# Page loads without a loop and a sample tile on four column tiles, in one step of a hybrid decoder

## The chip, the cores and the metric

The kernel runs on one core of one Trainium2 chip. The metric is the device time of one execution in microseconds (us). Three timed runs of the kernel before gave 1723.5, 1726.23 and 1726.19 us; their median is 1726.19 us. Lower is better.

## The reference

One decoder layer handles 1024 prompt tokens and 8 x 4 sample tokens (32 rows). What the change touches is cut out here:

```
def nsa_sample(q, cmp_kv, sel_kv, ..., cache_cmp, cache_sel, win_state, page_table, cmp_w):
    past_cmp = cache_cmp[page_table].reshape(db, past, N_KV, 2, HEAD_DIM)   # 8 sequences x 16 pages of 128 rows
    k_p, v_p = compress_blocks(past_cmp, *cmp_w)                            # blocks of 64 rows -> one key, one value
    o_cmp, imp = compressed_attention(q, k_c, v_c, pos)
    idx, valid = select_blocks(imp, pos)                                    # 16 best blocks by importance
    kv_past = cache_sel[phys, r_past % PAGE_SIZE, gi]                       # pages of the second cache
    ... selected and window attention, gates

def merge_and_ffn(x, conv_out, att_out, ...):
    mix = concat(rmsnorm(conv_out), rmsnorm(att_out)) @ w_out               # (1056, 1024) @ (1024, 1024)
    x = x + mix
    return x + hier_moe(rmsnorm(x, ln2), ...)
```

The page table is a row of 128 integers, 16 for each sample sequence; each names a page of 128 rows in the two caches. Before them stand the input projection (`mix_inputs`) and the convolution module, behind them the experts and the last normalization.

## The kernel before

All data are float32. The program is a row of blocks; at the end of each block all engines meet at a barrier, so a block lasts until its slowest engine is done. Tokens are worked in nine tiles: eight of 128 prompt rows (`NQ` = 8) and a ninth of the 32 sample rows.

1. Input stage, 0 to 321 us. Normalization, projection, convolution taps. GpSimd (POOL) does nothing between two memsets near 1 us and a first copy at 167 us (L609). SyncE (SP) loads inputs; the page table is the DMA of L269, into `page_row`. Near 54 us SP issues its last DMA there and then waits for landings.
2. Compression stage, 321 to 436 us. The 128 pages of `cache_cmp` are 128 KB each (128 partitions x 1 KB). They come in four batches q = 0..3 of 32 pages; `cmp_pages` lets SP load the even 16 and POOL the odd 16 of a batch. Two buffers: batches 0 and 1 go to free memory (batch 1 once the convolution's rows have been turned, `conv_turned`), batch 2 waits for the two products of batch 0 (`compressed` >= 2), batch 3 for those of batch 1 (`compressed` >= 4). SP also loads the weights, 2 MB for keys (`load_weights(0)`) ahead of its batch 0, and 2 MB for values behind it. On TensorE (PE) `compress(q, v)` multiplies a batch with the key weights (v = 0) or the value weights (v = 1), 64 matmul instructions each, L706; `blocks(q)` are small products behind. The order on PE is `compress` for q = 0, 1, 2, then `blocks(0)`, `blocks(1)`, `compress(3, 0)`, `blocks(2)`, `compress(3, 1)`, `blocks(3)`. Between its pages of batch 1 and those of batch 2, POOL does nine additions of 512 columns for the convolution (L831), and ScalarE (ACT) and VectorE (DVE) follow these.
3. Prompt attention, 436 to 732 us. SP loads the 64 pages of `cache_sel` of the first four sequences, POOL the value halves of 16 more.
4. Sample attention, 732 to 832 us, in two halves of four sequences. When the first half's scores stand (`s_scored`), SP loads the key halves of batches 0 and 2 of the second half and POOL those of batches 1 and 3 (`last_pages`, 64 KB a page); the second half's scores (L1279) need all four. When the first half is through (`sampled`), SP, POOL and ACT load the value halves of one batch each.
5. Mix stage, 832 to 1011 us. For each token tile: `turn_mix` transposes, `mix(t, 0)` and `mix(t, 1)` multiply with the left and the right half of `w_out` into PSUM banks 2 and 3 (L1489), DVE's `merge` adds the input row (L1592), ACT takes the squares (L1555), DVE scales (L1615), PE turns the result (`turn_h`, L1499), ACT and DVE copy it (L1564, L1624), PE multiplies with the router (L1511), DVE takes the logits (L1598). The scaled rows of the last tile can only be made when both of its merges are done.
6. Routing, experts and the last normalization, from 1011 us to the end.

A page load works as follows. A register must hold the page number. `value_load` is a load of one integer from `page_row` into a register, with a bounds check and address arithmetic (L645). In `load_pages` a loop runs four times; each round loads four numbers and then issues four DMAs (L648). In batches 2 and 3 the wait for `compressed` stands ahead of the loop, so ahead of the numbers too.

Of the kernel before, what the change touches and what calls it, by code (L numbers as in the profile page):

```python
# [132 lines left out]
def build(nc, a):  # L133

    _, const_at, const_small = const_table()
    with ExitStack() as ctx:
# [109 lines left out]
        tap_place = {what: n for n, what in enumerate([v for us in early_taps for v in us] + late_taps)}  # L246
        with nc.Block() as block:
            @block.sync
            def _(sp):
# [7 lines left out]
                for t in range(TILES):  # L257
# [22 lines left out]
                  .then_inc(sem("state_out"), 16)  # L280
                sp.wait_ge(sem("state_out"), 32)
# [358 lines left out]
        def load_pages(eng, cache, first, b, event, part=slice(0, 256), spare=None):  # L640


            into, step, base = (pages_flat, 256, b * PAGES * 256 + part.start) if spare is None else (spare, 128, 0)
            with eng.Fori(0, PAGES // 4) as s:
                places = [eng.value_load(page_row[0:1, bass.ds(s * 4 + (first + q), 1)],  # L645
                                         min_val=0, max_val=cache.shape[0] - 1) for q in range(4)]
                for q, place in enumerate(places):
                    eng.dma_start(into[:, bass.ds(s * (4 * step) + (base + q * step), part.stop - part.start)],  # L648
                                  cache[bass.ds(place, 1)].rearrange("a p n -> (a p) n")[:, part])\
                       .then_inc(sem(f"{event}{b}"), 16)  # L650
# [15 lines left out]
        pages_flat = flat(A1, 18688)  # L666
# [249 lines left out]
        with nc.Block() as block:  # L916
            @block.sync
            def _(sp):
                for b in range(4):
                    load_pages(sp, a["cache_sel"], b * PAGES, b, "sel_page")  # L920
# [138 lines left out]
            def _(pool):  # L1059
                load_pages(pool, a["cache_sel"], HALF + 3 * PAGES, 3, "sel_values", slice(P, 2 * P), last_values)  # L1060
# [159 lines left out]
        def last_pages(eng, event, part, batches):  # L1220
# [1029 lines left out]
```

## Time and profile before

| what | us |
|---|---|
| timed runs, median of three | 1726.19 |
| the profiled execution, its own time | 1724.38 |
| its span (first to last instruction) | 1722.5 |
| compression stage | 321 to 436 |
| sample attention | 732 to 832 |
| mix stage | 832 to 1011 |
| PE busy in the span | 1418.5 |
| DVE, ACT, POOL busy | 680.9, 371.5, 196.1 |

The profile is of one execution, whose time lies within the three timed ones. Times in rows are us from the start of the span, unless a row says ns. A row of the timeline gives start, duration, engine, line, operation, `out<-in`, shape, count, and in brackets how long the engine had been idle and who ended it. "SPq" and "POOLq" are the instruction sequencers of these engines. PEclk is the clock that was granted to TensorE, 1.00 being 2.4 GHz and 0.50 being 1.2 GHz. "DMA" is the busy share of the core's 16 DMA engines.

### The profile page before, as it was taken

To read this page: it belongs to the slowest core of one execution; us is meant where nothing else is said; L and a number is where in the kernel's file an instruction comes from. 1 tells how busy PE (TensorE), PEld (TensorE's weight loads), DVE (VectorE), ACT (ScalarE), POOL (GpSimd) and SP (SyncE) were. 2 spreads that over 40 slices of the span, in tenths; PEclk is the share of its full clock that TensorE was granted. 3 is DMA by queue.
4 is the path that set the end of the run, shared out by engine and by line. 5 is a ranking of instruction groups with operands and counts; after the bars stand their busy time and mean duration, and the time that the engine had idled before them with its cause. 6 is when DMAs were issued, how large, how long until landed. Compare 5 with 4: busy or idle time off the path is not lost. (4 is left out here: it accounts for less than half of the span.)

```text
span 1722.5 us, 22851 instructions
## 1 busy us (share of the span) xinstructions
PE 1418.5 (82%) x7480; PEld 830.2 (48%) x7480; DVE 680.9 (40%) x1314; ACT 371.5 (22%) x796; POOL 196.1 (11%) x348
## 2 busy tenths in 40 slices
PE   5999999478889888823599942999999999999950
PEld 4665445378656556511355521445444544454420
DVE  3497787501488777645122255001000100010008
ACT  4000111330366554430111100111111111111103
POOL 0000011362100000014000000011111111111111
PEclk8999999788589999966699975999999999999985
DMA  7500000474330000045311107699999999999917
GB/s 267 231 1 6 13 16 19 154 240 123 111 99 14 2 1 2 1 141 146 152 61 61 41 17 302 258 393 401 405 412 386 409 400 402 377 396 395 396 50 291
DMA packets 83021, 326.79 MB, mean 190 GB/s; under 512 B 12319, under 2 KB 48288, under 8 KB 64834
## 3 DMA queue, kind: packets, MB, share of 16 engines
q1 hardware_dynamic: 65130, 287.76, 42.7%
q0 software_dynamic: 15440, 37.09, 6.4%
q10 hardware_dynamic: 2384, 1.06, 0.2%
q8 instruction: 41, 0.67, 0.2%
q14 instruction: 26, 0.21, 0.0%
HBM read 311.20 MB, written 29.45 MB: 198 GB/s over the span
## 5 line engine op out<-in xcount | busy, mean ns | idle before, releaser
L1792 PE MATMUL ps<-arena 128*128 128x512 f32 x544 | 239.9, 597 | 0.0
L1792 PEld LDWEIGHTS ps<-arena 128*128 128x128 f32 x544 | 102.1, 190 | 136.9 <-issue 136.8
L521 DVE SCALAR_TENSOR_TENSOR arena<-arena 128x1024 f32<-128x1024 f32 x120 | 147.5, 1282 | 1.2
L1489 PE MATMUL ps<-arena 128*128 128x512 f32 (+1 forms) x288 | 129.6, 603 | 15.3 <-DVE arena L1584 15.3
L354 PE MATMUL ps<-arena 128*128 128x512 f32 (+1 forms) x384 | 141.2, 527 | 0.0
L1800 PE MATMUL ps<-arena 128*64 128x256 f32 x1088 | 121.2, 380 | 0.0
L308 PE MATMUL ps<-arena 128*128 128x352 f32 x384 | 117.5, 467 | 4.3 <-issue 3.9
L1844 PE MATMUL ps<-arena 128*128 128x512 f32 x272 | 119.6, 591 | 0.0
L1090 ACT ACTIVATE arena<-ps,arena 128x640 f32<-128x640 f32 (+7 forms) x128 | 89.9, 703 | 108.9 <-DVE arena L1167 101.9
L354 PEld LDWEIGHTS ps<-arena 128*128 128x128 f32 x384 | 72.0, 189 | 67.2 <-issue 61.6
L999 PE MATMUL ps<-arena 128*128 128x128 f32 x528 | 87.3, 289 | 20.4 <-DVE arena L1185 9.8
L1904 DVE TENSOR_TENSOR arena<-arena,ps 128x512 f32<-128x512 f32 x17 | 11.7, 689 | 226.8 <-PE ps L1792 226.8
L1800 PEld LDWEIGHTS ps<-arena 128*64 128x64 f32 x1088 | 75.9, 135 | 50.5 <-issue 12.9
L706 PE MATMUL ps<-arena 128*128 128x128 f32 (+1 forms) x512 | 69.2, 299 | 33.5 <-DMA arena<-in_cache_cmp 32.4
L308 PEld LDWEIGHTS ps<-arena 128*128 128x128 f32 x384 | 73.7, 193 | 46.5 <-issue 6.6
L1167 DVE TENSOR_REDUCE arena<-ps 128x1 f32<-128x640 f32 (+7 forms) x128 | 90.6, 708 | 4.4
L1489 PEld LDWEIGHTS ps<-arena 128*128 128x128 f32 (+1 forms) x288 | 51.5, 184 | 80.8 <-issue 80.7
L706 PEld LDWEIGHTS ps<-arena 128*128 128x128 f32 x512 | 68.3, 207 | 34.4 <-issue 34.3
L1013 PE MATMUL ps<-arena 128*64 128x128 f32 x1056 | 73.8, 281 | 9.2 <-ACT arena L1097 4.7
L999 PEld LDWEIGHTS ps<-arena 128*128 128x128 f32 x528 | 57.5, 143 | 46.0 <-issue 18.9
L1844 PEld LDWEIGHTS ps<-arena 128*128 128x128 f32 x272 | 50.2, 190 | 57.2 <-issue 57.2
L977 PE MATMUL ps<-arena 64*128 64x512 f32 (+3 forms) x384 | 76.9, 507 | 1.1 <-ACT arena L1077 0.7
(365 smaller groups left out, 1549.7 us busy)
## 6 DMA issues: line engine op xcount, KB each, us to landing
arena<-in_w_gate SPq DMA_DIRECT2D x34, 2048.0 KB, 9.8
arena<-in_w_up SPq DMA_DIRECT2D x34, 2048.0 KB, 14.3
arena<-in_w_down SPq DMA_DIRECT2D x34, 2048.0 KB, 13.8
arena<-in_x_prompt SPq DMA_DIRECT2D x16, 512.0 KB, 6.5
arena<-in_cache_cmp SPq DMA_DIRECT2D x64, 128.0 KB, 2.8
arena<-in_cache_cmp POOLq DMA_DIRECT2D x64, 128.0 KB, 2.9
arena<-in_cache_sel SPq DMA_DIRECT2D x64, 128.0 KB, 2.1
arena<-scratch_y SPq DMA_DIRECT2D x16, 512.0 KB, 5.8
```

The source lines that it names most:

```text
L308: mm = pe.matmul(ps[:, 4 + 2 * (u % 2) + half, 0:NW], w_conv[:, k, half * CH + c * P:half * CH + c * P + P], xT[:, k, j * NW:(j + 1) * NW] ...
L354: mm = pe.matmul(ps[:n, b + o // 512, 0:w], xT[:, k, t * P:t * P + n], w_tm[:, k, o:o + w], start=(k == 0), stop=(k == KT_ - 1))
L521: ins = dve.scalar_tensor_tensor(o, i, dw[:, c, j:j + 1], o, ALU.mult, ALU.add)
L706: mm = pe.matmul(ps[:, cmp_bank(q, v), 256 * v:256 * v + n], w_cmp1[:, v, l, :], pages[:, at:at + n // 4, 128 * v + 4 * l:128 * v + 4 * l ...
L977: mm = pe.matmul(ps[:, score_bank(p, g) + o // 4, 0:n], qT[64 * g:64 * g + 64, r, i * P:(i + 1) * P], kT[64 * g:64 * g + 64, w, (first + o ...
L999: mm = pe.transpose(ps[:, turn_bank("chunk", c), j * P:(j + 1) * P], probs_of(h, m)[:, (o + j) * P:(o + j + 1) * P], ident)
L1090: act.activation(probs_of(h, m), scores(p, g), ACT.Exp, bias=neg_max[:, h % 4:h % 4 + 1], accum_out=sums[:, i % 2, w, R * g + r:R * g + r ...
L1167: dve.tensor_reduce(neg_max[:, h % 4:h % 4 + 1], s, AX.X, ALU.max, negate=True)\
L1489: mm = pe.matmul(ps[:n, 2 + half, :], mixT[:, t % 2, k, 0:n], w_out[:, k, 512 * half:512 * half + 512], start=(k == 0), stop=(k == KT_ - 1))
L1792: mm = pe.matmul(ps[:, bank, :], xgT_l[:, k, :], w[LARGE][:, k, :], start=(k == 0), stop=(k == KT_ - 1))
L1800: mm = pe.matmul(ps[HF * h:HF * h + HF, bank, 0:HH], xgT_s[:, k, :], w[SMALL][:, k, HH * h:HH * h + HH], start=(k == 0), stop=(k == KT_ - ...
L1844: mm = pe.matmul(ps[:, half, :], hidT_l[:, q // 2, q % 2, :], w_down[LARGE][:, q // 2, q % 2, 512 * half:512 * half + 512], start=(q == 0) ...
```

## The change

- `load_pages` has no loop any more. `page_places` loads sixteen numbers into sixteen registers, one after the other, and `load_pages` then issues sixteen DMAs.
- The numbers of batches 0 and 1 of the compression stage are loaded in the input stage: by SP behind its last DMA there, by POOL behind its two memsets. Each holds 32 registers until the compression stage.
- In batches 2 and 3 the numbers are loaded ahead of the wait for `compressed`.
- All other page loads (stages 3 and 4) load sixteen numbers where the loop stood, then issue.
- In the mix stage the sample tile's product is made by `mix_last`: one pass over `w_out` with four products side by side, each of 32 columns of the array and 256 columns of `w_out`, all into bank 2. ACT and DVE copy two quarters each to their place, and DVE adds the input to the whole row of 1024 in one instruction.

```
+        def page_places(eng, cache, first):
+            return [eng.value_load(page_row[0:1, first + q:first + q + 1], min_val=0, max_val=cache.shape[0] - 1)
+                    for q in range(PAGES)]
+        def load_pages(eng, cache, places, into, event, part=slice(0, 256)):
+            for q, place in enumerate(places):
+                eng.dma_start(into(q), cache[bass.ds(place, 1)].rearrange("a p n -> (a p) n")[:, part])\
+                   .then_inc(sem(event), 16)
+        first_places = {}
 ...
             def _(sp):                                       # input stage, behind the last DMA
+                sp.wait_ge(sem("page_table_in"), 16)
+                for q in range(2):
+                    first_places[q, 0] = page_places(sp, a["cache_cmp"], 2 * q * PAGES)
 ...
             def _(pool):                                     # input stage, behind the memsets
+                pool.wait_ge(sem("page_table_in"), 16)
+                for q in range(2):
+                    first_places[q, 1] = page_places(pool, a["cache_cmp"], (2 * q + 1) * PAGES)
 ...
-        def load_pages(eng, cache, first, b, event, part=slice(0, 256), spare=None):
-            into, step, base = (pages_flat, 256, b * PAGES * 256 + part.start) if spare is None else (spare, 128, 0)
-            with eng.Fori(0, PAGES // 4) as s:
-                places = [eng.value_load(page_row[0:1, bass.ds(s * 4 + (first + q), 1)], ...) for q in range(4)]
-                for q, place in enumerate(places):
-                    eng.dma_start(into[:, bass.ds(s * (4 * step) + (base + q * step), part.stop - part.start)], ...)
         def cmp_pages(eng, q, odd):
-            if q == 0:
-                eng.wait_ge(sem("page_table_in"), 16)
+            if q < 2:
+                places = first_places[q, odd]
+            else:
+                places = page_places(eng, a["cache_cmp"], (2 * q + odd) * PAGES)
             if q == 1:
                 eng.wait_ge(sem("conv_turned"), TILES)
             if q >= 2:
                 eng.wait_ge(sem("compressed"), 2 * (q - 1))
-            load_pages(eng, a["cache_cmp"], (2 * q + odd) * PAGES, 2 * (q % 2) + odd, "cmp_page")
+            b = 2 * (q % 2) + odd
+            load_pages(eng, a["cache_cmp"], places, lambda k: pages[:, PAGES * b + k, :], f"cmp_page{b}")
 ...
+                def mix_last():                              # TensorE
+                    n = rows(NQ)
+                    pe.wait_ge(sem("merged0"), NQ)
+                    for k in range(KT_):
+                        for q in range(4):
+                            mm = pe.matmul(ps[n * q:n * q + n, 2, 0:256], mixT[:, NQ % 2, k, 0:n],
+                                           w_out[:, k, 256 * q:256 * q + 256], start=(k == 0), stop=(k == KT_ - 1),
+                                           tile_position=(0, n * q))
+                    mm.then_inc(sem("last_mixed"), 1)
 ...
+                    if q == NQ:                              # ScalarE
+                        act.wait_ge(sem("last_mixed"), 1)
+                        for part in range(2):
+                            ins = act.activation(x_res[:n, q, 256 * part:256 * part + 256],
+                                                 ps[n * part:n * part + n, 2, 0:256], ACT.Copy)
+                        ins.then_inc(sem("last_copied"), 1)
 ...
+                def merge_last():                            # VectorE
+                    n = rows(NQ)
+                    dve.wait_ge(sem("last_mixed"), 1)
+                    for part in range(2, 4):
+                        ins = dve.tensor_copy(x_res[:n, NQ, 256 * part:256 * part + 256],
+                                              ps[n * part:n * part + n, 2, 0:256])
+                    ins.then_inc(sem("merged0"), 1)
+                    dve.wait_ge(sem("merged0"), TILES)
+                    dve.wait_ge(sem("last_copied"), 1)
+                    dve.wait_ge(sem(f"xt_in{NQ % 2}"), 16 * (NQ // 2 + 1))
+                    dve.tensor_tensor(x_res[:n, NQ, :], x_res[:n, NQ, :], xt[:n, NQ % 2, :], ALU.add)\
+                       .then_inc(sem("merged1"), 1)
```

How this moves instructions is shown at three places. First SP at the start of the compression stage, before; `in_w_cmp` are the key weights, L645 is the loading of numbers (TENSOR_LOAD and its check and arithmetic), L648 the issue of a page:

```order
21 L668 UNCONDITIONAL_BRANCH [waits barrier_Pool_Activation_PE_DVE_SP_release]
22 L671 DMA arena<-in_w_cmp 128x4096
23 L644 UNCONDITIONAL_BRANCH [waits page_table_in]
24 L644 ISA
25 L645 TENSOR_LOAD page_row
26 L645 ISA x3
27 L645 TENSOR_LOAD page_row
28 L645 ISA x3
29 L645 TENSOR_LOAD page_row
30 L645 ISA x3
```

The same place after (L249 is the loading of numbers now, L255 the issue):

```order
85 L677 UNCONDITIONAL_BRANCH [waits barrier_Pool_Activation_PE_DVE_SP_release]
86 L680 DMA arena<-in_w_cmp 128x4096
87 L255 ISA
88 L255 DMA arena<-in_cache_cmp 128x256
89 L255 ISA
90 L255 DMA arena<-in_cache_cmp 128x256
```

Behind the weights the pages follow directly; the 32 number loads of batches 0 and 1 stand in the input stage. Second, SP ahead of batch 2, after; before, the wait stood on the loop's branch ahead of the first number:

```order
183 L249 TENSOR_LOAD page_row
184 L249 ISA x2
185 L249 TENSOR_LOAD page_row
186 L249 ISA x2
187 L255 ISA [waits compressed]
188 L255 DMA arena<-in_cache_cmp 128x256
```

The wait now stands behind all sixteen numbers, on the first issue. One number costs a load and two further instructions, where the loop had three for most. Third, PE at the end of the mix stage, before (L1489 is `mix`, L1499 `turn_h`, L1511 `router`):

```order
417 L1489 MATMUL ps<-arena 128x512 x8
418 L1511 MATMUL ps<-arena 128x36 x8
419 L1489 MATMUL ps<-arena 32x512 x8
420 L1499 MATMUL ps<-arena 128x128 x8
421 L1489 MATMUL ps<-arena 32x512 x8
422 L1511 MATMUL ps<-arena 128x36 x8
423 L1499 MATMUL ps<-arena 128x32 x8
424 L1511 MATMUL ps<-arena 32x36 x8
```

and after (L1502, L1522, L1534 are the same three, L1512 is `mix_last`):

```order
417 L1502 MATMUL ps<-arena 128x512 x8
418 L1534 MATMUL ps<-arena 128x36 x8
419 L1512 MATMUL ps<-arena 32x256 x32
420 L1522 MATMUL ps<-arena 128x128 x8
421 L1534 MATMUL ps<-arena 128x36 x8
422 L1522 MATMUL ps<-arena 128x32 x8
423 L1534 MATMUL ps<-arena 32x36 x8
```

Two groups of eight wide products became one group of 32 products of half the width, and nothing of the sample tile's product is left behind `turn_h` of tile 7. On DVE the merges of the last tile stand in a row now, behind the copy of tile 7's turned rows (L1673):

```order
867 L1664 SCALAR_TENSOR_TENSOR arena<-arena 128x1024
868 L1673 COPY arena<-ps 128x512
869 L1632 COPY arena<-ps 32x256 x2
870 L1638 TENSOR_TENSOR arena<-arena 32x1024
871 L1644 COPY arena<-ps 128x36
872 L1658 RECIPROCAL arena<-arena 32x1
873 L1664 SCALAR_TENSOR_TENSOR arena<-arena 32x1024
```

Before, a merge of 32x512 stood ahead of that copy and a second one behind it.

## Rows read from the trace of the kernel before

**Rows 1.** The page, its first line.
```profile
span 1722.5 us, 22851 instructions
```
**Rows 2.** Timeline, compression stage: start, us, engine, line.
```profile
321.16 0.35 SPq L671 DMA_DIRECT2D arena<-in_w_cmp  x1
324.74 17.43 SPq L648 DMA_DIRECT2D arena<-in_cache_cmp  x16
340.96 2.44 POOL L648 DMA_DIRECT2D arena<-in_cache_cmp  x4 [2.92 <-issue]
...
342.39 0.36 SPq L671 DMA_DIRECT2D arena<-in_w_cmp  x1
...
352.14 16.58 PE L706 MATMUL ps<-arena 128*128 128x128 f32 x128 [24.64 <-DMA arena<-in_cache_cmp]
...
367.62 11.10 POOL L831 TENSOR_TENSOR arena<-arena 128x512 f32<-128x512 f32 x9
369.86 18.29 PE L706 MATMUL ps<-arena 128*128 128x164 f32 x128 [1.14 <-issue]
393.05 16.61 PE L706 MATMUL ps<-arena 128*128 128x128 f32 x128 [4.90 <-DMA arena<-in_cache_cmp]
...
415.25 10.25 PE L706 MATMUL ps<-arena 128*128 128x128 f32 x64 [2.86 <-DMA arena<-in_cache_cmp]
...
426.39 7.42 PE L706 MATMUL ps<-arena 128*128 128x128 f32 x64
```
**Rows 3.** Windows: stretch, length, busy of PE, PEld, DVE, ACT, POOL; PEclk, DMA, GB/s.
```profile
323.00:327.00 4.00, 4.00 (x26) 3.99 (x25) 3.85 (x9) 3.07 (x6) 1.91 (x4) 0.66 0.93 389
334.00:338.00 4.00, 0.00 (x0) 0.00 (x0) 3.86 (x8) 0.00 (x0) 2.11 (x4) 0.50 0.65 210
380.00:386.00 6.00, 6.00 (x44) 6.00 (x44) 0.00 (x0) 5.75 (x18) 5.14 (x10) 1.00 0.90 272
```
**Rows 4.** SP in 368:376, L645 and L648; then POOL's landings in 342:343.5.
```profile
L645 SPq TENSOR_LOAD <-page_row x8: 263/264/273, 368.9 to 376.0; - x8
L648 SPq DMA_DIRECT2D arena<-in_cache_cmp x4: 342/343/347, 371.6 to 373.3; - x4
...
DMA to landing us min/median/max: 3.0/7.2/9.1
```
**Rows 5.** DMA queues, 318 to 436 us: packets, MB, share.
```profile
q1 hardware_dynamic: 9936, 13.14, 34.6%
q0 software_dynamic: 3232, 8.52, 23.3%
```
**Rows 6.** Timeline, sample attention, SP, POOL, DVE and PE.
```profile
751.27 0.39 SPq L1235 DMA_DIRECT2D arena<-in_state_win_use  x1
...
754.66 39.02 SPq L648 DMA_DIRECT2D arena<-in_cache_sel  x32
...
790.47 5.39 DVE L1395 SCALAR_TENSOR_TENSOR arena<-arena 128x512 f32<-128x512 f32 x8
791.96 2.44 POOL L648 DMA_DIRECT2D arena<-in_cache_sel  x4 [2.89 <-issue]
...
799.10 5.83 PE L1279 MATMUL ps<-arena 128*32 128x512 f32 x32 [15.79 <-DMA arena<-in_cache_sel]
```
**Rows 7.** Timeline: a product on four column tiles, a copy, an addition, the mix stage's end.
```profile
306.62 4.59 PE L359 MATMUL ps<-arena 128*32 128x326 f32 x64
...
434.95 0.43 DVE L816 COPY arena<-ps 128x256 f32<-128x256 f32 x1 [21.27 <-PE ps L728]
...
751.95 1.23 DVE L1383 TENSOR_TENSOR arena<-arena 128x1024 f32<-128x1024 f32 x1
...
988.84 7.05 PE L1489 MATMUL ps<-arena 128*32 128x512 f32 x16
...
997.02 0.69 DVE L1624 COPY arena<-ps 128x512 f32<-128x512 f32 x1 [0.41 <-PE ps L1499]
...
1004.78 1.06 ACT L1555 ACTIVATE arena<-arena 32x1024 f32<-32x1024 f32 x1 [7.16 <-DVE arena L1592]
```

More of the change, by code:

```diff
@@ L659, in cmp_pages @@
                 eng.wait_ge(sem("compressed"), 2 * (q - 1))
-            load_pages(eng, a["cache_cmp"], (2 * q + odd) * PAGES, 2 * (q % 2) + odd, "cmp_page")
+            b = 2 * (q % 2) + odd
+            load_pages(eng, a["cache_cmp"], places, lambda k: pages[:, PAGES * b + k, :], f"cmp_page{b}")
         def cmp_bank(q, v):
             return 4 if (q, v) == (3, 1) else 4 + q
-        pages_flat = flat(A1, 18688)
         with nc.Block() as block:
@@ L919, in _ @@
                 for b in range(4):
-                    load_pages(sp, a["cache_sel"], b * PAGES, b, "sel_page")
+                    load_pages(sp, a["cache_sel"], page_places(sp, a["cache_sel"], b * PAGES),
+                               lambda q, b=b: pages[:, PAGES * b + q, :], f"sel_page{b}")
             @block.tensor
@@ L1059, in _ @@
             def _(pool):
-                load_pages(pool, a["cache_sel"], HALF + 3 * PAGES, 3, "sel_values", slice(P, 2 * P), last_values)
+                load_pages(pool, a["cache_sel"], page_places(pool, a["cache_sel"], HALF + 3 * PAGES),
+                           lambda q: last_values[:, P * q:P * q + P], "sel_values3", slice(P, 2 * P))
             @block.scalar
@@ L1218, in build, with last_pages @@
         att_ss, att_sd, att_rs = stat(TILES), stat(TILES), stat(TILES)
-        def last_pages(eng, event, part, batches):
+        def last_pages(eng, event, part, batches, places=None):
             for b in batches:
-                load_pages(eng, a["cache_sel"], HALF + b * PAGES, b, event, part)
+                places = places or page_places(eng, a["cache_sel"], HALF + b * PAGES)
+                load_pages(eng, a["cache_sel"], places, lambda q: pages[:, PAGES * b + q, part], f"{event}{b}", part)
+                places = None
         with nc.Block() as block:
@@ L1519, in _ @@
                     pe.wait_ge(sem("mixT_dve"), t + 1)
-                    mix(t, 0)
+                    if t < NQ:
+                        mix(t, 0)
+                    else:
+                        mix_last()
                     if t + 1 < TILES:
@@ L1524, in _ @@
                         turn_h(t - 1)
-                    mix(t, 1)
+                    if t < NQ:
+                        mix(t, 1)
                     if t >= 1:
@@ L1604, in _ @@
                     q, n = t - 1, rows(t - 1)
-                    merge(q, 1)
+                    if q < NQ:
+                        merge(q, 1)
+                    else:
+                        merge_last()
                     if q >= 1:
@@ L1616, in _ @@
                                              ln2_g[:n, :], ALU.mult, ALU.mult).then_inc(sem("h_ready"), 1)
-                    if t < TILES:
+                    if t < NQ:
                         merge(t, 0)
```

5 lines of the change are left out of this document (removed).

## The prediction

> **What bounds the kernel now.** I read the page first, for the span [rows 1] and for the slices in which TensorE is not full. Then the list of waits of PE, which names three places where PE waits for a transfer; then the timeline of those places, and of SP and POOL there, to see what issued the transfer late. The stages end in barriers, so a gain in one is kept in full unless the next waits for something older; the next stages wait for nothing that was issued before their barrier, except pages that come hundreds of us early.
>
> In the compression stage PE stands idle 24.64 us ahead of batch 0, 4.90 ahead of batch 2, 2.86 ahead of batch 3 and 1.14 ahead of batch 1 [rows 2]. Up to the first product only SP's and POOL's loops are at work: SP issued the key weights at 321.16 but its first page at 324.74, needed 17.43 for sixteen, and POOL issued four pages in 2.44 us and then did nothing for 2.92, four times [rows 2]. The DMA engines were 0.65 busy at 334 to 338 [rows 3]. So issuing sets the pace there, not the transfer. The last of POOL's pages was issued beside the 2 MB of value weights of 342.39 and took up to 9.1 us to land [rows 4], which gives the 352.14 at which PE starts.
>
> **The price of an issue.** SP's numbers of one round start at 368.9 and its first page is issued at 371.6 [rows 4]: 2.7 us for four numbers and what leads to the issue, 0.63 each, and 0.61 without the one address instruction that the change drops: 9.7 us for sixteen. Four pages start from 371.6 to 373.3 [rows 4], 0.57 apart: 9.1 us for sixteen on SP. POOL: 2.44 / 4 = 0.61 [rows 2], 9.8 for sixteen. A batch with its numbers is thus 18.8 on SP and 19.5 on POOL, against 4 x (2.44 + 2.92) = 21.4 before; with the numbers read ahead it is 9.1 and 9.8.
>
> **Numbers in the input stage.** 32 numbers are 19.4 us on each engine. POOL is idle there until 167 us and SP is through near 54, so they are hidden; if that cover were gone they would cost the stage 19 us.
>
> **Compression stage.** Batches 0 and 1 are now limited by the transfer. Rates: with weights in it 389 GB/s [rows 3]; pages alone 272 at a share of 0.90 [rows 3], 302 at a full share. Weights of 2.10 MB take 5.4 us, a batch of 32 pages (4.19 MB) 13.9. From 323, when data flow, key weights and batch 0 take 19.3: 342.3, with 1 us of landing 343.3. That holds if SP's and POOL's pages share the engines evenly. POOL, however, issues batch 1 right behind batch 0 (all 32 by 341), and its packets are 8.52 MB / 3232 = 2.6 KB against 1.3 KB on SP's queue [rows 5]. If POOL's pages went first altogether, SP's half of batch 0 would end at 323 + 5.4 + 13.9 + 7.0 = 349.3, and batch 0 would be in at 350.3. I keep both ends.
>
> The Trainium skill (DMA: Bandwidth & Descriptors, Queues, rings and completion order) says that each DMA engine goes round between queue rows packet by packet. By that rule the larger packets win and the start lies near 350; by an even split of bytes it is 343. The landing of 9.1 us beside the weights [rows 4] agrees with the rule.
>
> It makes little difference at the end. Value weights, two small loads (128 and 160 KB, 1 us) and what is left of batch 1 are in by 323 + 2 x 5.4 + 1 + 2 x 13.9 = 362.6, landed 363.6, in either order. Even split: PE works batch 0 from 343.3 for 16.6 [rows 2] to 359.9, waits 3.7, and starts batch 1 at 363.6 with a clock that has fallen: behind a wait of 2.86 us 64 instructions took 10.25, without a wait 7.42 [rows 2], so a short wait costs 2.8 more. Batch 1 ends at 363.6 + 18.3 + 2.8 = 384.7. POOL first: 350.3 + 16.6 + 18.3 = 385.2. I take 385.
>
> Batch 2: POOL is through with batch 1 at 341, then four small output DMAs and the nine additions, 11.10 us [rows 2], to about 355, then sixteen numbers to 364.5. It may issue when batch 0's products are done (360 to 367) and is through by 377; the transfer of 13.9 from 369 ends at 383, before 385. Batch 2 starts at 385 without a wait, hot: 2 x 7.42 = 14.8 [rows 2], to 399.8. Batch 3: numbers are read while batch 1 is multiplied, issue from 385 to 395, transfer from 386 to 400 or 401. PE has `blocks(0)` and `blocks(1)` between, 2.7 us (409.66 to 412.39, the ends of batch 2 and of the start less its wait [rows 2]), to 402.5. So batch 3 arrives 1 or 2 us before it is wanted: the tightest place. Its first product starts at 402.5 against 415.25, 12.75 earlier, and takes 7.42 for 10.25, 2.83 less: 15.6. I take 15.0, for the tight place. Bounds: 17.5 (nothing waits at all), 9 (batch 3 late by 3 and cold, 2.8).
>
> **Prompt attention.** SP's 64 pages and POOL's 16 are wanted more than 200 us later: nothing.
>
> **Sample attention.** The second half's scores start at 799.10, released by the last key page; POOL issued its last ones from 791.96 for 2.44, SP ended at 754.66 + 39.02 = 793.7 [rows 6]. Now the numbers are not read ahead: they follow `s_scored` at about 751.3, and the first page comes 6 us later than before. The last: SP 751.7 + 2 x 18.8 = 789.3, POOL about 751.5 + 0.7 + 2 x 19.5 = 791.2 against 794.4. Gain 3.2. DVE is free at 790.47 + 5.39 = 795.9 [rows 6] and wants the scores 7 us after PE's start, so all of it counts. The value halves behind it come earlier by at least as much. Bounds 0 (SP's 1 MB window load, issued 4 us earlier, crowds the last pages) and 4.5.
>
> **Mix stage.** Removed: two groups of 7.05 us [rows 7]. Added: 64 instructions of 256 columns on four column tiles. The same form with 326 columns took 4.59 [rows 7]; 4.59 x 256 / 326 = 3.6. `mix_last` runs from 988.84 to 992.4. Then on the path: transposes of tile 7, 1.1 (from 995.89, the end of the product, to the copy at 997.02), DVE's copy of them 0.69, two copies of a quarter at 0.43, the addition of 1024 columns 1.23 [rows 7] and about 0.2 of hand-over: ACT's squares start at 996.5 instead of 1004.78, and all behind them is as before. Gain 8.2. The new waits: DVE's `merge_last` holds the logits of tile 7, which nobody needs before the stage's end; ACT's two copies run beside DVE's. Bounds 7 (copies at 0.69 each) and 9.
>
> **Sum.** 15.0 + 3.2 + 8.2 = 26.4 from the profiled execution's 1724.38 (span 1722.5 [rows 1], 1.9 around it): 1698.0. The median of the timed runs is 1.8 above the profiled one, so I forecast 1700.
>
> **Rivals.**
> - *The DMA engines are the bound already.* Pages run at 272 GB/s, not 302. Batch 1 is then in at 323 + 10.8 + 1 + 30.8 + 1 = 366.6, PE is cold, batch 1 ends at 387.7, batch 3 has landed at 405 for 405.2: gain 12.3 instead of 15, or less by one cold start (9.5). The kernel: 1703 to 1706. For it: 0.90 to 0.93 busy where pages or weights run. Against: 0.65 at 334 to 338 [rows 3]. The Trainium skill (DMA: Bandwidth & Descriptors, Issuing engines are not separate DMA queues) says that initiating from several engines saves only the sequencers' time, usually small beside the transfer; that rule speaks for this rival and against the change, and the trace agrees with it at 380 to 386 us and not at 334 to 338.
> - *POOL is held while it issues.* With 32 of its pages queued it may only finish issuing when the queue drains, near 358. Then additions and numbers follow to 381.5, its half of batch 2 lands at 394, PE waits 9 and goes cold, and batch 3's gain shrinks to 4.5. The kernel: 1710. For it: no row shows so many pages queued on it. Against: with fewer queued, each issue took 0.61.
> - *The four tiles do not run side by side.* 64 x 0.215 = 13.8 us (half of 7.05 / 16 each), 10.2 more than forecast: the mix stage loses 2 us, the kernel stands at 1710. Against: the row with 326 columns.
> - *Slower: straight code starves the sequencers.* SP has 803 rows of program for 320, POOL 629 for 279. Where the loop ran the same few instructions, each batch is now some 80 new ones, to be fetched past full DMA engines. Six batches lie on the path (four in the compression stage, two in the sample attention). If each stood for 9.1 us, the worst landing [rows 4], that is 54.6, less 26.4: 28 slower, 1754. It decides from 4.4 us a batch, and makes the kernel slower by 0.2% from 5.0. Against: PE, whose code is all straight, waited 1.14 at the one such place.
> - *It does not do what it says:* if number loads were put back behind the barrier, batches 0 and 1 would start 10 us later, and about 5 would be left of the 15: 1710. The order of SP's rows excludes it.
>
> **How the numbers follow.** Forecast 0.62; DMA-bound 0.18; POOL held 0.11; tiles not side by side 0.03; slower 0.03; the rest, smaller gains for unknown reasons, 0.03. The likeliest case alone spans 1694 to 1704 (stage bounds 17.5 + 4.5 + 9 on one side, 12 + 1 + 7.5 on the other). Low end 1692, by all upper bounds at once: 1726.2 - 31 = 1695, and 3 for spread between runs. High end 1712, which takes in the two cases of 1710. A change under 0.2% (3.5 us) could not be told from none. Faster 0.95, same 0.02, slower 0.03.
>
> **What would show it.** In the new profile: PE's first product of the compression stage at 343 to 350 and its wait there 16 to 23 us for 24.64; batch 1 at 363 to 367; batches 2 and 3 with no wait, and 7.4 us for each half of batch 3; a DMA share above 0.9 from 323 to 362. The second half's scores at 796; `mix_last` in 3.6 us and the mix stage 8 us shorter. I am wrong if PE waits ahead of batch 2 (POOL held), if it waits more than 3 us ahead of batch 3, or if the stages sum to less than 20.

## The result, and the profile after

| | median us | runs | range |
|---|---|---|---|
| before | 1724.85 | 4 | 1722.64 to 1726.23 |
| changed | 1696.46 | 4 | 1695.42 to 1699.43 |

The ratio is 0.9838, 95% interval [0.9826, 0.9851]: 28.4 us faster, where 26.4 were forecast. The profiled execution of the changed kernel took 1699.43 us, the slowest of its four, span 1697.7. A second set of five runs, timed beside `e8` and `e9` below, gave 1697.09, ratio 0.9842 [0.9828, 0.9855].

Compression stage of the changed kernel, timeline: start, us, engine, line. L255 is the page DMA, L680 a load of weights, L715 the product of a batch, L840 POOL's additions. They answer to [rows 2].

```profile
320.88 0.35 SPq L680 DMA_DIRECT2D arena<-in_w_cmp  x1
321.45 15.45 SPq L255 DMA_DIRECT2D arena<-in_cache_cmp  x16
321.56 5.23 POOL L255 DMA_DIRECT2D arena<-in_cache_cmp  x9 [4.69 <-POOLq L260]
327.15 13.40 POOL L255 DMA_DIRECT2D arena<-in_cache_cmp  x23 [0.35 <-issue]
336.95 1.03 SPq L680 DMA_DIRECT2D arena<-in_w_cmp  x1
339.97 14.27 SPq L255 DMA_DIRECT2D arena<-in_cache_cmp  x16
343.21 11.10 POOL L840 TENSOR_TENSOR arena<-arena 128x512 f32<-128x512 f32 x9
347.29 49.50 PE L715 MATMUL ps<-arena 128*128 128x128 f32 x384 [20.08 <-DMA arena<-in_cache_cmp]
...
364.59 29.27 SPq L255 DMA_DIRECT2D arena<-in_cache_cmp  x32
365.10 9.33 POOL L255 DMA_DIRECT2D arena<-in_cache_cmp  x16 [10.79 <-PE ps L715]
...
399.48 7.40 PE L715 MATMUL ps<-arena 128*128 128x128 f32 x64
407.77 7.42 PE L715 MATMUL ps<-arena 128*128 128x128 f32 x64
```

The three batches stand in one row of 384 instructions, since nothing parts them: of the four waits of [rows 2] one is left, 20.08 us for 24.64. The last halves have no bracket, and the first of them takes 7.40 where it took 10.25. Both engines now issue from the first moment of the stage, POOL all 32 pages of two batches in a row.

Windows of the same stage, columns as in [rows 3]:

```profile
331.00:335.00 4.00, 0.00 (x0) 0.00 (x0) 3.87 (x7) 0.80 (x1) 3.66 (x8) 0.65 1.05 346
343.00:347.00 4.00, 0.00 (x0) 0.00 (x0) 0.00 (x0) 1.30 (x3) 3.89 (x5) 0.50 1.13 401
355.00:359.00 4.00, 4.00 (x39) 4.00 (x37) 0.00 (x0) 3.84 (x11) 0.00 (x0) 1.00 0.95 301
359.00:363.00 4.00, 4.00 (x38) 4.00 (x37) 0.00 (x0) 3.89 (x9) 0.00 (x0) 1.00 0.03 11
375.00:379.00 4.00, 4.00 (x30) 4.00 (x30) 0.00 (x0) 0.00 (x0) 0.00 (x0) 1.00 1.04 341
```

Where [rows 3] had a share of 0.65 and 210 GB/s the engines are full. Pages alone move at 325 GB/s (371 to 375 us) to 350 (339 to 343). By 359 the engines are idle: everything up to the end of batch 1 is in.

Sample attention, SP, DVE and PE (answers to [rows 6]; L1292 is the scores, L1408 and L1414 are VectorE's choice and its first use of the scores):

```profile
733.32 0.37 SPq L1248 DMA_DIRECT2D arena<-in_state_win_use  x1
743.00 26.02 SPq L255 DMA_DIRECT2D arena<-in_cache_sel  x32
...
772.75 5.39 DVE L1408 SCALAR_TENSOR_TENSOR arena<-arena 128x512 f32<-128x512 f32 x8
776.75 6.61 PE L1292 MATMUL ps<-arena 128*32 128x512 f32 x32 [11.16 <-DMA arena<-in_cache_sel]
784.49 2.48 DVE L1414 TENSOR_TENSOR arena<-ps,arena 128x512 f32<-128x512 f32 x4 [6.34 <-PE ps L1301]
```

DVE is free at 778.14 and waits 6.34 more. Before, the last of these rows stood 73.94 us after its stage's start, with a wait of 10.20:

```profile
806.06 2.48 DVE L1401 TENSOR_TENSOR arena<-ps,arena 128x512 f32<-128x512 f32 x4 [10.20 <-PE ps L1288]
```

End of the mix stage (answers to [rows 7]; L1512 is `mix_last`, L1632 DVE's two quarters, L1638 the addition of the whole row, L1588 ACT's squares):

```profile
968.02 3.66 PE L1512 MATMUL ps<-arena 128*32 128x256 f32 x64
971.61 1.16 PE L1522 MATMUL ps<-arena 128*128 128x128 f32 x8
972.81 0.69 DVE L1673 COPY arena<-ps 128x512 f32<-128x512 f32 x1 [2.60 <-PE ps L1522]
973.30 0.75 ACT L1583 ACTIVATE arena<-ps 32x256 f32<-32x256 f32 x2
973.53 0.86 DVE L1632 COPY arena<-ps 32x256 f32<-32x256 f32 x2
974.42 1.22 DVE L1638 TENSOR_TENSOR arena<-arena 32x1024 f32<-32x1024 f32 x1
975.73 1.06 ACT L1588 ACTIVATE arena<-arena 32x1024 f32<-32x1024 f32 x1 [1.68 <-DVE arena L1638]
```

The start of each stage's first instruction (PE's for the prompt attention, SP's DMA for the others), in the profiled executions of both kernels:

| starts at, us | before | changed | gained in the stage ahead |
|---|---|---|---|
| compression | 321.16 | 320.88 | 0.3 |
| prompt attention | 436.01 | 417.39 | 18.3 |
| sample attention | 732.12 | 713.52 | 0.0 |
| mix | 832.18 | 810.95 | 2.6 |
| routing | 1011.20 | 982.14 | 7.8 |
| end of span | 1722.5 | 1697.7 | -4.3 |

The last row is code that the change doesn't touch. From routing to the end took 711.3 us here before, and 712.7 to 716.1 in the eleven profiled executions of the changed kernel and the experiments. The spread is nearly as large as the loss, but all eleven lie above the one value from before, by 1.4 to 4.8 us.

One number of this table is not typical. The sample attention takes 97.4 us here (100.1 before), but 95.6 to 96.5 in the six other profiled executions with the same code in that stage (`e1` to `e5` and the second set), so its gain is 2.6 in this execution and 3.6 to 4.5 in those.

### The profile page after: what moved, and what is told of

It reads as the page before. It is cut to its first block and busy times, and to the rows that moved or that the text cites. A ratio compares the mean times of both kernels' runs of the same rounds, so it can differ in the third digit from the quotient of the medians.

```text
span 1697.7 us, 22399 instructions
## 1 busy us (share of the span) xinstructions
PE 1408.0 (83%) x7512; PEld 826.5 (49%) x7512; DVE 681.6 (40%) x1315; ACT 372.4 (22%) x797; POOL 195.7 (12%) x347
## 5 line engine op out<-in xcount | busy, mean ns | idle before, releaser
L1841 PE MATMUL ps<-arena 128*128 128x512 f32 x544 | 240.2, 598 | 0.0
L1841 PEld LDWEIGHTS ps<-arena 128*128 128x128 f32 x544 | 102.1, 190 | 137.1 <-issue 137.0
L370 PE MATMUL ps<-arena 128*128 128x512 f32 (+1 forms) x384 | 141.2, 527 | 0.0
L1502 PE MATMUL ps<-arena 128*128 128x512 f32 x256 | 115.6, 605 | 15.7 <-DVE arena L1617 15.7
L1893 PE MATMUL ps<-arena 128*128 128x512 f32 x272 | 119.7, 592 | 1.2 <-DMA arena<-scratch_h,ints 1.2
L370 PEld LDWEIGHTS ps<-arena 128*128 128x128 f32 x384 | 72.0, 189 | 67.1 <-issue 61.6
L324 PEld LDWEIGHTS ps<-arena 128*128 128x128 f32 x384 | 73.7, 193 | 45.6 <-issue 5.8
L1502 PEld LDWEIGHTS ps<-arena 128*128 128x128 f32 x256 | 48.2, 193 | 72.1 <-issue 72.1
L715 PE MATMUL ps<-arena 128*128 128x128 f32 (+1 forms) x512 | 64.3, 287 | 20.1 <-DMA arena<-in_cache_cmp 20.1
L1009 PEld LDWEIGHTS ps<-arena 128*128 128x128 f32 x528 | 58.0, 144 | 46.4 <-issue 19.4
L1893 PEld LDWEIGHTS ps<-arena 128*128 128x128 f32 x272 | 50.2, 190 | 58.6 <-issue 57.2
L255 POOL DMA_DIRECT2D arena<-in_cache_sel x64 | 34.9, 546 | 361.5 <-issue 358.5
```

Source lines behind the costliest of these rows:

```text
L324: mm = pe.matmul(ps[:, 4 + 2 * (u % 2) + half, 0:NW], w_conv[:, k, half * CH + c * P:half * CH + c * P + P], xT[:, k, j * NW:(j + 1) * NW] ...
L370: mm = pe.matmul(ps[:n, b + o // 512, 0:w], xT[:, k, t * P:t * P + n], w_tm[:, k, o:o + w], start=(k == 0), stop=(k == KT_ - 1))
L1009: mm = pe.transpose(ps[:, turn_bank("chunk", c), j * P:(j + 1) * P], probs_of(h, m)[:, (o + j) * P:(o + j + 1) * P], ident)
L1502: mm = pe.matmul(ps[:n, 2 + half, :], mixT[:, t % 2, k, 0:n], w_out[:, k, 512 * half:512 * half + 512], start=(k == 0), stop=(k == KT_ - 1))
L1841: mm = pe.matmul(ps[:, bank, :], xgT_l[:, k, :], w[LARGE][:, k, :], start=(k == 0), stop=(k == KT_ - 1))
L1893: mm = pe.matmul(ps[:, half, :], hidT_l[:, q // 2, q % 2, :], w_down[LARGE][:, q // 2, q % 2, 512 * half:512 * half + 512], start=(q == 0) ...
```

## The experiments

All kernels start from the changed one; times are medians of timed runs, before being 1723.7 to 1725.5 in each set. `e1` to `e4`, `e5` to `e7` and `e8` to `e10` ran on three chips, so a difference of medians across sets is uncertain by a microsecond or two; the ratios are each to the kernel before on the same chip. "Stage" is the compression stage, from SP's load of the key weights (or PE's first instruction, 0.03 later) to PE's first product of the prompt attention: 96.5 us in the changed kernel, 114.9 before.

**Which part of the page loads is worth what.** `e1_numbers_late`: the input stage loads no numbers, batches 0 and 1 load theirs in the stage.

```
-            if q < 2:
-                places = first_places[q, odd]
-            else:
-                places = page_places(eng, a["cache_cmp"], (2 * q + odd) * PAGES)
+            places = page_places(eng, a["cache_cmp"], (2 * q + odd) * PAGES)
```

> The changed kernel, but the numbers of batches 0 and 1 are read in the compression stage, sixteen ahead of each batch, and not in the input stage. Theory A (the compression stage is bound by the DMA engines once the loop is gone, so a later start of the issue is mostly made good): the first page is issued near 331 instead of 321.5, batch 0 is issued by 341, and PE's first product starts at 346 to 350 as it does now (347.3); batch 1 is issued by 361 and lands at 363 to 364, just when PE wants it. Cost 0 to 5 us: ratio to the kernel before 0.984 to 0.987. Theory B (the early numbers are worth their own time): PE starts 9.7 us later, at 357, and the kernel stands 8 to 10 us above the changed one, ratio 0.989 to 0.990.

Measured 1699.97 (ratio 0.9856 [0.9832, 0.9881]), 3.5 over the changed kernel. The interval overlaps that of the changed kernel, so by time alone this is no clear difference; the stage in the trace shows it:

```profile
330.06 9.63 POOL L255 DMA_DIRECT2D arena<-in_cache_cmp  x16 [13.76 <-issue]
330.50 8.64 SPq L255 DMA_DIRECT2D arena<-in_cache_cmp  x16
345.97 17.23 PE L708 MATMUL ps<-arena 128*128 128x128 f32 x128 [19.55 <-DMA arena<-in_cache_cmp]
...
365.85 33.97 PE L708 MATMUL ps<-arena 128*128 128x164 f32 x256 [2.65 <-DMA arena<-in_cache_cmp]
```

Counted from the stage's start (320.38), the first pages are issued 9.0 us later on POOL and 9.6 on SP, and yet the first product starts no later: after 25.6 us, 26.4 in the changed kernel. So something there takes the DMA engines' time from batch 0 (below). Here batch 1 pays, with 2.65 us of wait, and the stage takes 100.3 us (320.38 to 420.71). The early numbers, the most visible part of the change, are worth 3.8 of the stage's 18.3 us in these two traces.

`e2_numbers_behind_wait`: the numbers of batches 2 and 3 are loaded behind the wait for `compressed`, as before the change.

```
             if q >= 2:
                 eng.wait_ge(sem("compressed"), 2 * (q - 1))
+                places = page_places(eng, a["cache_cmp"], (2 * q + odd) * PAGES)
```

> The changed kernel, but the numbers of batches 2 and 3 of the compression stage are read behind the wait for the buffer, as in the loop, and not ahead of it. Theory A (each batch has just enough time, so 9.7 us of numbers on the way uncover a wait): batch 2 is issued from 373.5 to 383 and lands at 386 to 388 against 382 when PE wants it; PE waits 4 to 5 us and the next product runs 1.8 to 2.8 longer at the lower clock; batch 3 is then just in time. Cost 6 to 8 us, ratio 0.987 to 0.989. Theory B (only the issue rate counts, buffers are free early enough): no wait, ratio 0.984 as now.

Measured 1707.69 (0.9896 [0.9873, 0.9918]), 11.2 over the changed kernel by medians and 10.0 by the ratios. PE waits ahead of batch 2:

```profile
374.32 9.33 POOL L255 DMA_DIRECT2D arena<-in_cache_cmp  x16 [19.45 <-PE ps L714]
389.18 16.84 PE L714 MATMUL ps<-arena 128*128 128x128 f32 x128 [6.55 <-DMA arena<-in_cache_cmp]
```

POOL begins at 374.32 for 365.10, and the 9.2 us go through to the end: the stage takes 105.9 us (321.08 to 426.93), 9.3 more. This is the largest single part of the change in this stage. The rest of the 11.2 stands in the prompt attention, 298.8 us for 296.1 (more on it under `e7`).

`e3_both`: both edits. 

> The changed kernel with both of these undone: sixteen numbers directly ahead of each batch's issue and behind its wait, no loop. What is left of the change in this stage is the missing loop and its order (sixteen numbers, then sixteen pages). Theory A: PE starts at 346 to 350; batch 2 lands 4 to 5 us late and PE is cold behind it; cost against the changed kernel 7 to 11 us, ratio 0.988 to 0.990. If early numbers and numbers ahead of the wait are worth their own time each (theory B) it is 18 us, ratio 0.994.

Measured 1708.58 (0.9905 [0.9884, 0.9927]), 12.1 over the changed kernel; the stage takes 109.9 us (319.72 to 429.62). In it the two parts add up (3.8 + 9.3 for 13.4); by medians they make 3.5 + 11.2 for 12.1, which is within the spread of such differences. Against 114.9 before, what is left, straight code and sixteen numbers in a row in place of four, is worth 5.0 us of the stage.

**The mix stage.** `e4_mix_before`: the mix stage as before the change, two passes for the sample tile. 

> The changed kernel with the mix stage of the kernel before. Theory A: the mix stage is on the path and ends in a barrier, so this costs what the traces show between their barriers, 7.8 us: ratio 0.988 to 0.989. Rival: part of the mix stage's gain is given back in the expert stage, whose span was 4.3 us longer in the profile of the changed kernel; then it costs 3.5 to 5 us, ratio 0.986 to 0.987.

Measured 1704.24 (0.988 [0.986, 0.99]), 7.8 over the changed kernel. Its first pass over `w_out` for the sample tile:

```profile
967.06 7.05 PE L1502 MATMUL ps<-arena 128*32 128x512 f32 x16
```

From mix to routing it takes 179.2 us (810.21 to 989.40), the changed kernel 171.2, before 179.0. Together with the table that settles the term.

**Who goes ahead in the queue.** By 347 us the changed kernel had moved 8.8 MB (the sum of the windows from 323), but weights and batch 0 are 6.3: some 2.5 MB of later data went ahead, 2.1 of them POOL's batch 1, since POOL's queue had moved 4.31 MB, both of its batches, by 347.5 us. The two queues in 334 to 338 us (packets, MB, share), when SP's still held batch 0 and POOL had issued half of its batch 1:

```profile
q0 software_dynamic: 356, 0.96, 70.1%
q1 hardware_dynamic: 470, 0.43, 35.5%
```

POOL's queue (q0) moved 0.96 MB in fewer packets than SP's (q1) needed for 0.43: its packets are 2.7 KB, SP's 0.9. `e5_adds_first` keeps POOL's batch 1 out of the way:

```
                 cmp_pages(pool, 0, 1)
-                cmp_pages(pool, 1, 1)
-                pool.dma_start(out["out8"], state_p[:TAPS - 1]).then_inc(sem("conv_out"), 16)
...
                 for t in range(TILES):
...
+                cmp_pages(pool, 1, 1)
                 cmp_pages(pool, 2, 1)
+                pool.dma_start(out["out8"], state_p[:TAPS - 1]).then_inc(sem("conv_out"), 16)
...
                 cmp_pages(pool, 3, 1)
```

> POOL issues its half of batch 0, then makes its nine additions, then issues its halves of batches 1 and 2, then the five small output transfers, then its half of batch 3. Theory A: in the changed kernel POOL's 16 loads of batch 1 take bandwidth from SP's half of batch 0, so the first product starts at 347.3 us though only 6.3 MB (weights and batch 0) are needed and 8.8 MB had moved by then; with the additions in between, the first product starts between 341 and 343 us. The end of the stage moves less, since SP has the numbers of batch 2 only at about 364.4 us whatever POOL does: 2 to 4 us under the changed kernel, ratio about 0.982. Rival B: the bytes that SP's own queue moves decide, and POOL's queue takes nothing from it: the first product still starts at 347 us and the time is that of the changed kernel, or 1 to 3 us over it, as POOL's half of batch 1 comes later.

Measured 1695.64 (0.9841 [0.9828, 0.9855]): no difference that can be told. Its stage starts at 319.20:

```profile
319.77 12.56 SPq L255 DMA_DIRECT2D arena<-in_cache_cmp  x16
...
330.40 1.42 POOL L835 TENSOR_TENSOR arena<-arena 128x512 f32<-128x512 f32 x1 [0.76 <-DVE arena L806]
...
339.17 16.34 PE L715 MATMUL ps<-arena 128*128 128x128 f32 x128 [14.25 <-DMA arena<-in_cache_cmp]
...
348.58 8.71 POOL L255 DMA_DIRECT2D arena<-in_cache_cmp  x16
...
361.42 35.22 PE L715 MATMUL ps<-arena 128*128 128x164 f32 x256 [5.91 <-DMA arena<-in_cache_cmp]
```

The mechanism of theory A is shown: the first product comes 20.0 us after the stage's start for 26.4, and the wait is 14.25 for 20.08. Rival B's 347 fell. The gain that A forecast didn't come; the stage even takes 98.4 us (319.20 to 417.63) for 96.5. A left two things out. The additions are fed by DVE, whose pairs of instructions come every 2.13 us when POOL adds beside it, so POOL had its batch 1 out only from 348.58, and the wait stood ahead of batch 1 instead. And in that wait of 5.91 the granted clock fell:

```profile
363.00:367.00 4.00, 4.00 (x17) 4.00 (x16) 1.03 (x2) 0.00 (x0) 0.55 (x2) 0.52 0.58 181
```

The 256 products of batches 1 and 2 took 35.22 us, where `e8` below, with a wait of 1.83 and a clock of 1.00, took 32.61. A's bound, that SP has the numbers of batch 2 only at 364.4, fell too: SP issued it from 355.69.

This also explains `e1`. There POOL issues batch 1 from 348.48, behind the first product, so nothing overtakes; its first product comes 5.6 us later than that of `e5`. In the changed kernel the early numbers gain about as much at the start, and the overtaking takes it away.

**The second half of the key pages.** `e6_sample_early`: SP and POOL load the 32 numbers each of the sample attention's key pages ahead of their wait for `s_scored`.

```
+                keys_at = [page_places(sp, a["cache_sel"], HALF + b * PAGES) for b in (0, 2)]
                 sp.wait_ge(sem("s_scored"), 1)
...
-                last_pages(sp, "sel_keys", slice(0, P), (0, 2))
+                for b, places in zip((0, 2), keys_at):
+                    last_pages(sp, "sel_keys", slice(0, P), (b,), places)
```

> The numbers of the 32 key pages of the sample attention are read ahead of the wait for the sample scores on SP and POOL, instead of behind it. Theory A: the key pages start 9 to 10 us earlier (733.6 instead of 743 us on the changed kernel's scale), the scores of TensorE are ready before VectorE has ended its choice at 778.1 us, and VectorE's wait of 6.3 us for them goes: 4 to 6 us under the changed kernel, ratio about 0.981. Rival B: the pages wait for the DMA engines, which both queues fill, or the page that comes last is still one of the values: 1 us or less.

Measured 1689.91 (0.9799 [0.9786, 0.9813]), 6.5 under the changed kernel's 1696.46 and 5.7 under `e5`, which has the changed kernel's sample attention and ran in the same set; the interval touches neither of theirs. SP, DVE and PE there:

```profile
732.02 18.05 SPq L255 DMA_DIRECT2D arena<-in_cache_sel  x32
...
763.91 3.66 PE L1296 MATMUL ps<-arena 128*32 128x512 f32 x32
...
771.15 5.39 DVE L1412 SCALAR_TENSOR_TENSOR arena<-arena 128x512 f32<-128x512 f32 x8
776.58 2.48 DVE L1418 TENSOR_TENSOR arena<-ps,arena 128x512 f32<-128x512 f32 x4
```

PE has no wait for a page and DVE none for PE; the sample attention takes 91.2 us (712.30 to 803.54) for 97.4 in the profile of the changed kernel and 95.6 to 96.5 in the six other ones. Theory A held in what moves: the pages start earlier and the waits go. Its size of DVE's wait, 6.3, isn't typical: `e2` to `e4` have 5.9 to 6.2, but `e1`, `e5` and the second set only 1.5 to 1.7, since DVE is free later there. In the second set:

```profile
782.36 2.48 DVE L1414 TENSOR_TENSOR arena<-ps,arena 128x512 f32<-128x512 f32 x4 [1.52 <-PE ps L1301]
```

The change loads these numbers in straight code but behind the wait; ahead of it they are worth 4.4 to 6.2 us more, by which trace is compared.

`e7_best`: both of the last two. 

> Both of the preceding edits. If each theory A holds they add up, since the stages lie apart: 6 to 10 us under the changed kernel, ratio 0.978 to 0.980. If both rivals hold: the time of the changed kernel, ratio 0.984.

Measured 1694.43 (0.9827 [0.9812, 0.9841]): neither theory. It is 2.0 under the changed kernel, whose interval overlaps its own, and 4.5 over `e6`. Its stage takes 98.3 us (319.86 to 418.19) where that of `e6` takes 96.4, the wait ahead of batch 1 being 5.67; this is what the edit of `e5` costs in both. The prompt attention takes 297.6 us for 295.0 in `e5` and `e6`, and from routing on it is 716.1 for 713.8; the two stages between are 2.0 us shorter. The first sixteen products of the prompt attention took 2.98 us for 1.94, at the lower clock. Three of the twelve profiled executions have such a start (`e2` 2.53, `e7` 2.98, `e8` 3.08), and their prompt attentions, 297.6 to 298.8 us, are longer than the nine others (295.0 to 297.3). What lets the clock fall there no run shows. By medians `e7` misses the sum of `e5` and `e6` by 5.3 us, most of it unexplained.

**Half the additions first.** `e8_adds_split4`: from `e6`, POOL makes four additions between its halves of batches 0 and 1, and the output DMAs behind the last addition. `e9_adds_split2`: two additions (`t == 2`).

```
                 for t in range(TILES):
+                    if t == 4:
+                        cmp_pages(pool, 1, 1)
```

> On top of e6_sample_early (1689.9 us): POOL issues its half of batch 0, makes four of its nine additions, issues its half of batch 1, makes the other five, then the five small output transfers, batches 2 and 3. Theory A (from e5_adds_first: the wait moved from batch 0 to batch 1 because VectorE paces the additions at 2.13 us each, so POOL was held until 348.6 us): four additions hold POOL until about 339 us only, the first product still starts near 340 us, POOL's half of batch 1 is in by about 353 us, ahead of the need at 356, and the stage ends 4 to 8 us earlier than in e6: 1682 to 1686 us, ratio 0.975 to 0.978. Rival B: the DMA engines set the pace, with 10.5 MB to move by the start of the second batch at no more than 345 GB/s: what starts earlier is waited for later, and the time is that of e6, 1689 to 1691 us.

> As e8_adds_split4, with two additions ahead of POOL's half of batch 1 instead of four. POOL issues batch 1 from about 335 us. Theory A: part of the overtaking is back, the first product starts at 342 to 344 us, and the time lies between e6 and e8, 1685 to 1688 us. Rival B: as for e8, that of e6.

Measured 1685.94 (0.9781 [0.9768, 0.9794]) and 1687.03 (0.9788 [0.9775, 0.9802]): 4.0 and 2.9 under `e6`, which ran in another set and whose interval overlaps theirs. So the gain rests on the traces: the stage takes 92.5 and 93.1 us, against 96.2 to 96.6 in the four executions that have POOL's batches 0 and 1 in a row and early numbers throughout (changed, `e4`, `e6`, second set). The stage of `e8`, which starts at 320.71:

```profile
339.76 8.96 POOL L255 DMA_DIRECT2D arena<-in_cache_cmp  x16
...
340.54 16.94 PE L715 MATMUL ps<-arena 128*128 128x128 f32 x128 [13.56 <-DMA arena<-in_cache_cmp]
359.32 32.61 PE L715 MATMUL ps<-arena 128*128 128x164 f32 x256 [1.83 <-issue]
```

Theory A of `e8` has the time (1682 to 1686) at its edge, but not its reason whole: batch 1 was to be in by 353, and PE could start it only at 359.32. The bracket there names no transfer; that PE waited for the last pages is read from the windows of `e8`, in which the engines empty just then:

```profile
357.00:359.00 2.00, 0.49 (x5) 0.29 (x3) 0.00 (x0) 1.91 (x7) 0.49 (x1) 1.00 0.80 267
359.00:360.00 1.00, 0.68 (x5) 0.71 (x6) 0.00 (x0) 0.97 (x4) 0.03 (x1) 1.00 0.09 25
```

In the changed kernel too the engines ran until 359 and then stood still, and in `e9` batch 1 began 38.8 us after the stage's start, as in `e8` (38.6). So two bounds meet here: in none of these three orders were the transfers up to the end of batch 1 done sooner (rival B's part), and the order decides only whether PE is through with batch 0 by then. In the changed kernel batch 1 began inside the row of 384, at about 347.29 + 16.94 = 364.2, if batch 0 took what it took in `e8`; in `e8` at 359.3. That is 4.9 us, and the stage got 3.9 shorter (92.5 for 96.4 in `e6`). `e9` started its first product 20.1 us after the stage's start, no later than `e8` (19.8): what POOL issues from 334.6 on no longer overtakes, and my 342 to 344 was wrong.

`e10_changed_again`, the changed kernel beside these two, is the second set of the first section. 

> The changed kernel once more, beside the two above, so that differences of a few us are read from runs on one chip: 1695 to 1699 us, ratio 0.983 to 0.985.

`e8_adds_split4` is the best version found: in the same set, 11.15 us under the changed kernel (1697.09) and 37.7 under the one before (1723.65). It isn't told apart from `e9`.

## Why the prediction was right

The mechanisms held stage by stage. That the gain came within 2 us of the forecast is in part luck: in the traces the compression stage gave 3.3 more than its term, the two others 1.0 less together, and of the 29.1 us gained up to routing the medians show 28.4. The measured 1696.46 lies 3.5 under the forecast 1700; 1.3 of that is the kernel before, 1724.85 and not 1726.19 in the final set.

- *What bounds the start: issuing, not transfer.* Right. PE's wait is 20.08 (16 to 23 expected), the DMA share 0.94 to 1.13 from 323 to 359.
- *Start between an even split (343.3) and POOL first (350.3).* Right as bounds: 347.29. With the 346 GB/s measured at 331 to 335 the same two sums give 341.5 and 347.6, so the start lies where all of POOL's batch 1 goes first; `e5` shows the overtaking (6.4 us earlier without it). The prediction argued it from packets of 2.6 KB against 1.3 KB. The 1.3 has the weights in it [rows 5]; pages alone are 0.9 KB on SP's queue. That the size of packets is the cause isn't shown: every run moves the same pages on the same two queues, so none parts the size of packets from the queue that they are on. The Trainium skill (DMA: Bandwidth & Descriptors, Queues, rings and completion order) says that each DMA engine goes round between queue rows packet by packet, by which the larger packets would carry more bytes. The trace agrees in direction: 356 packets and 0.96 MB on POOL's queue against 470 and 0.43 MB on SP's.
- *Compression stage 15.0.* The term that was mis-sized: 18.3 measured, outside the bounds of 9 to 17.5. The step that failed is the rate of pages, 302 GB/s at a full share, scaled up from a row of 272 at 0.90 [rows 3]; full, they ran at 325 to 350, and the kernel before had such a window too (383 to 387 us: a share of 1.00, 325 GB/s). The low rate put the start with POOL first at 350.3; it came 3.0 earlier, nothing behind it waited, and PE ended batch 2 at 396.8 instead of 399.8: 3.0 of the 3.3 us. The branch with an even split, a wait of 3.7 ahead of batch 1 and 2.8 for a fallen clock, didn't happen; batch 1 was in by 359 and not at 363.6.
- *Batch 3, "the tightest place".* It started at 399.48, with no wait and at the full clock: 7.40 for 10.25, as forecast.
- *POOL's part of batch 2.* Numbers were ready ahead of `compressed`, as forecast, and POOL issued at 365.10, released by PE. But the forecast had the numbers behind the nine additions, at 364.5, just in time. They ran beside the additions (343.21 to 354.3) and were in at 351.7. `e2` shows what loading them ahead of the wait is worth: 9.3 us of the stage. The last five numbers' checks on POOL's sequencer (L249):

```profile
L249 POOLq SEQ_ASSERT  x5: 18/18/18, 349.2 to 351.7; - x5
```

- *Sample attention 3.2.* 2.6 by the stages' starts and 3.0 by DVE's first use of the scores (relative to its stage, 73.94 before, 70.97 after), but 3.6 to 4.5 by the stage's length in the six other traces. The forecast lies between. No run puts the loop back in this stage alone, so the term rests on traces, with only one of the kernel before.
- *Mix stage 8.2.* 7.8 by the stages' starts, and 7.8 from `e4`. `mix_last` took 3.66 for my 3.6.
- *Rivals.* DMA-bound at 272 GB/s: fell by the windows. POOL held while it issues: fell, 23 pages in 13.40 us, 0.58 each. Tiles not side by side (13.8 us, 14.1 by its own row): fell, 3.66. Starved sequencers: fell, in the compression stage neither engine has a gap over 0.36 us between the issues of a batch. What I had not thought of is that SP is held: sixteen issues took 15.45 where [rows 4] gave 9.1. It cost nothing visible here: SP's numbers of batch 2 ran from 354.8 to 363.4 and it issued at 364.59, while PE was through with batch 0 at about 364.2.
- *A side remark that was wrong.* Were the early numbers absent, "about 5 would be left of the 15". `e1` keeps 14.5 of 18.3 us in the stage (100.3 for 114.9). A late start of batch 0 is mostly made good, since the engines run full behind it and POOL's batch 1 no longer goes ahead of batch 0.
- *Behind the stages.* 29.1 us had been gained up to routing and 24.8 at the end of this execution. The forecast had all of it kept. By medians 28.4 were kept; whether the expert stage gives back a part each time (all eleven traces are longer there than the one before) or only varies, the traces don't settle. The forecast's likeliest span, 1694 to 1704, was taken from the profiled 1724.4; from the median, as the 1700 is, it would be 1695 to 1706. It makes no difference to the outcome.

## What to carry to other kernels

When both issuers queue work for a buffer ahead of need, look at the bytes moved by the time the first consumer starts: if they exceed what it needs, a later transfer has overtaken, and part of an issuer's other work belongs between its first and second batch. Loading addresses ahead of a wait was worth most at the waits that lie in the middle of a pipeline (9.3 us at batches 2 and 3, 4.4 to 6.2 in the sample attention), least at its start (3.8, since a later transfer overtook). A transfer rate should be taken from a window in which the engines are full. And a stage's length should be read from more than one profile: the sample attention of the same code took 95.6 to 97.4 us, a spread of 1.8 beside a term of 2.6 to 4.5.

## What the runs showed of the hardware

- Pages of 128 KB from two full queues ran at 325 to 350 GB/s in windows of 4 us; as the loops issued them, at 210 (334 to 338 us) and 272 (380 to 386).
- With both queues full POOL's carried 0.96 MB in 356 packets and SP's 0.43 MB in 470 (334 to 338 us, the changed kernel).
- With the DMA engines full, SP's issues of pages stretched from 0.57 to 0.97 us each (15.45 for sixteen), POOL's stayed at 0.58. In `e1`, whose engines were 0.70 busy in the first two thirds of SP's issues (from 330.50), sixteen took 8.64:

```profile
330.00:336.00 6.00, 0.00 (x0) 0.00 (x0) 5.79 (x11) 1.22 (x1) 5.94 (x10) 0.59 0.70 208
```

- POOL's pages of batch 1, issued behind its own half of batch 0, delayed the first product of batch 0 by 6.4 us; issued 14.7 us after the stage's start (`e9`) they delayed nothing.
- While POOL added, DVE's multiplications of two tiles of 512 columns (L806) took 1.63 us, and 0.69 while POOL only issued DMAs (`e5` and the changed kernel):

```profile
335.00 1.63 DVE L806 TENSOR_TENSOR arena<-arena 128x512 f32<-128x512 f32 x1
```

```profile
335.01 0.69 DVE L806 TENSOR_TENSOR arena<-arena 128x512 f32<-128x512 f32 x1
```
